# Odd mixer's output projection made from split products, with its parts spread over the attention units; two small reorderings elsewhere

## The reference, cut to what matters

```
# even layer: state space group and differential attention side by side
y_a = mamba2_group(...)            # gated, RMS-normalized over 1024 features
y_b = diff_attention_group(...)    # 8 heads x 4 query blocks = 32 units
h = h + concat([y_a, y_b]) @ ev_w_out          # 2048 -> 1024
h = h + swiglu(rms_norm(h, norm_ffn[0]), ...)
# odd layer
u, c_q, c_kv, k_rope = split(rms_norm(h) @ od_w_in)
y_c = s5_group(u, ...)             # state space, 512 wide, ends in a gated linear unit
y_d = mla_group(c_q, c_kv, ...)    # q = rms(c_q) @ w_uq, kv = rms(c_kv) @ w_ukv; 8 heads x 4 blocks
h = h + concat([y_c, y_d]) @ od_w_out          # 1024 -> 1024
h = h + swiglu(rms_norm(h, norm_ffn[1]), ...)
out = rms_norm(h, norm_final)
```

## Time and profile before

| | us |
|---|---|
| median of 3 runs (lowest to highest) | 3118.67 (3118.42 to 3120.23) |
| the profiled execution | 3117.89 |
| its span | 3115.7 |
| PE busy in the span | 2978.9 (96%) |
| DVE, ACT, POOL busy | 1382.1, 795.4, 1297.4 |

### The profile page before, as it was taken

One profiled execution on the slowest core, in us unless ns is written; L12 is line 12 of the kernel. 1 busy time (PEld: TensorE's weight loads), 2 busy tenths in 40 slices (PEclk: granted clock), 3 DMA queues, 4 the chain that ended last, 5 costly groups with the idle time before them and its releaser, 6 DMA issues.

```text
span 3115.7 us, 36425 instructions
## 1 busy us (share of the span) xinstructions
PE 2978.9 (96%) x14436; PEld 2265.3 (73%) x14436; DVE 1382.1 (44%) x2281; ACT 795.4 (26%) x1491; POOL 1297.4 (42%) x1070
## 2 busy tenths in 40 slices
PE   8999999999989999998899988999999889999997
PEld 5878777778778777776687655788787545478886
DVE  3312455666463122433746676523726844321113
ACT  3011222221130122211326233232223124232222
POOL 2434223223435633457565543744545300054443
PEclk8999999999999999999999998999999889999999
DMA  7111112223222211123321111232324200232322
GB/s 268 41 41 61 61 62 88 64 76 109 91 71 82 75 51 51 51 81 106 97 75 51 59 50 59 76 99 82 99 91 132 69 29 14 81 108 88 101 84 78
DMA packets 244819, 245.76 MB, mean 79 GB/s; under 512 B 5376, under 2 KB 234624, under 8 KB 244032
## 3 DMA queue, kind: packets, MB, share of 16 engines
q1 hardware_dynamic: 243360, 239.92, 24.0%
q0 software_dynamic: 1312, 3.80, 0.4%
HBM read 235.19 MB, written 7.34 MB: 78 GB/s over the span
## 4 chain that ended last, share of the span: by engine, by line
PE 85%; DVE 10%; issue 1%; ACT 1%; POOL 1%; SPq 1%; DMA 1%; DVEq 0%; POOLq 0%; ACTq 0%
PE psum L921 21%; PE psum L923 20%; PE psum L922 20%; PE psum L1178 4%; PE psum L1280 3%; PE psum L1147 2%; PE psum L1115 2%; PE psum L1116 1%; DVE columns L2540 1%; PE psum L1127 1%; PE psum L1077 1%; POOL columns L3232 1%; PE psum L1631 1%; PE psum L1182 1%; PE psum L1426 1%
## 5 line engine op out<-in xcount | busy, mean ns | idle before, releaser
L921 PE MATMUL psum<-columns,columns 128*128 128x512 f32 (+1 forms) x3400 | 1333.7, 392 | 55.2 <-POOL columns L3232 13.6
L923 PE MATMUL psum<-columns,columns 128*128 128x512 f32 (+1 forms) x3400 | 1243.4, 366 | 0.0
L922 PE MATMUL psum<-columns,columns 128*128 128x512 f32 (+1 forms) x3400 | 1242.1, 365 | 0.0
L3232 POOL TENSOR_TENSOR columns<-columns,columns 128x512 fp32r<-128x512 f32 (+1 forms) x660 | 883.8, 1369 | 437.4 <-ACT columns L1799 404.6
L3228 POOL TENSOR_TENSOR columns<-columns,columns 128x512 fp32r<-128x512 f32 x376 | 392.8, 1075 | 1282.7 <-PE psum L923 989.5
L921 PEld LDWEIGHTS psum<-columns,columns 128*128 128x128 f32 x3400 | 646.1, 190 | 236.1 <-issue 99.5
L922 PEld LDWEIGHTS psum<-columns,columns 128*128 128x128 f32 x3400 | 647.2, 190 | 119.8 <-issue 28.5
L923 PEld LDWEIGHTS psum<-columns,columns 128*128 128x128 f32 x3400 | 645.2, 190 | 109.4
L1799 ACT ACTIVATE columns<-columns 128x1024 fp32r<-128x1024 f32 (+2 forms) x154 | 136.8, 936 | 170.4 <-PE psum L923 166.0
L2540 DVE SCALAR_TENSOR_TENSOR columns<-columns,columns,columns 128x256 f32<-128x256 f32 x224 | 149.8, 714 | 0.5
L2522 DVE SCALAR_TENSOR_TENSOR columns<-columns,psum 128x512 f32<-128x512 f32 x80 | 54.8, 685 | 173.6 <-PE psum L1178 169.2
(11 more groups left out here) (405 smaller groups left out, 2805.7 us busy)
## 6 DMA issues: line engine op xcount, KB each, us to landing
columns<-in_w_merge SPq DMA_DIRECT2D x32, 1024.0 KB, 6.1
columns<-in_w_ada SPq DMA_DIRECT2D x24, 1024.0 KB, 5.3
columns<-in_w_in SPq DMA_DIRECT2D x22, 1024.0 KB, 5.3
columns<-in_ev_w_in SPq DMA_DIRECT2D x22, 1024.0 KB, 5.2
columns<-in_ffn_gate SPq DMA_DIRECT2D x22, 1024.0 KB, 5.3
columns<-in_ffn_up SPq DMA_DIRECT2D x22, 1024.0 KB, 5.3
columns<-in_ffn_down SPq DMA_DIRECT2D x16, 768.0 KB, 4.7
columns<-in_ffn_down SPq DMA_DIRECT2D x16, 640.0 KB, 4.3
```

The lines of the kernel that those rows point to most:

```text
L921: mm(dst, weights(0, k), moving(0, k), start=start and k == 0, stop=False)
L922: mm(dst, weights(0, k), moving(1, k), start=False, stop=False)
L923: last = mm(dst, weights(1, k), moving(0, k), start=False, stop=stop and k == k_tiles - 1)
L3232: last = g.tensor_tensor(low[:, c], raw[:, c], high[:, c].bitcast(F32), ALU.subtract)
```

## The change

**The output projection becomes a split product and begins earlier.** `od_out` leaves the list of unsplit stages, so its 64 slices are three fp32r matmuls each, its four panels are split by POOL (both parts), and its input is split tile by tile. ACT writes the high part of each tile (`out_tile`) at the odd mixer's places 12, 20, 22 to 25 and 28, and of the last one behind place 34. The low parts of `yd` are DVE's (`out_low`, places 13, 21, 29 and the end), those of `yc` are POOL's, between the splits of the first and the second panel. From place 28 on, two slices follow each place on PE (14 in all: tiles 4, 5, 0, 1, 2, 3, 6 of outputs 0 and 1). Behind the last place come slice 7 of outputs 0 and 1, then outputs 2 to 7 with all eight. The PSUM banks are 2 to 5 in place of 0 to 3. SP reloads the residual ahead of the third panel in place of the second.

```diff
-WHOLE = ("ada", "od_low", "glu", "od_out")
+WHOLE = ("ada", "od_low", "glu")
+OUT_HIGHS = (4, 5, 0, 1, 2, 3, 6, 7)
+EARLY_AT = 28
+EARLY = [(n, k) for k in OUT_HIGHS[0:7] for n in range(2)]
...
-        program += some("unit", u) + beside.get(u, [])
+        program += some("unit", u) + beside.get(u, []) + some("early", *range(2 * (u - EARLY_AT), 2 * (u - EARLY_AT) + 2) if u >= EARLY_AT else ())
...
# SP
-                if j == 1:
+                if j == 2:
                     sp.wait_ge(x_spilled, 32)
                     sp.wait_ge(scored2, 64)
                     sp.dma_start(xT[:, :, 0:SEQ], x_dram).then_inc(x_loaded, 16)
...
# PE
+                def out_product(n, k, start, stop):
+                    w = split_ready(PANEL0["od_out"] + n // 2)
+                    if n == 0 and k < 4:
+                        pe.wait_ge(y_split, KD + k + 1)
+                    elif n == 0:
+                        pe.wait_ge(od_split, KD + k - 3)
+                    low = yc_low[:, k, :] if k < 4 else yd_low[:, k - 4, :]
+                    src, o = (out_high[:, k, :], low), (2 + n % 4) * BANK
+                    return product(psum[:, o:o + SEQ], ..., lambda part, _: src[part], 1, start, stop)
...
                 pe.wait_ge(p2_ready, 64)
-                    feature_job(n % 4, w, n % 2 * P, lambda k: yc[:, k, :] if k < 4 else yd[:, k - 4, :]).then_inc(gemm_done, 1)
+                    tiles = OUT_HIGHS[7:] if n < 2 else OUT_HIGHS
+                    for k in tiles:
+                        last = out_product(n, k, n >= 2 and k == tiles[0], k == tiles[-1])
+                    last.then_inc(gemm_done, 1)
...
# ACT
+                        if i in (12, 20, 28):
+                            out_tile(4 + (i - 12) // 8)
+                        elif 22 <= i < 26:
+                            out_tile(i - 22)
+                out_tile(7)
...
# POOL
+            for n in range(4):
+                q = PANEL0["od_out"] + n
+                pool.wait_ge(gemm_done, DONE[q - 2 if n >= 2 else PANEL0["od_in"] + 3 + n])
+                split((SPLITS[q] - 1) % 2, KD * PANEL, *panel(q), SPLITS[q])
+                if n == 0:
+                    for k in range(4):
+                        pool.wait_ge(od_high, KD + OUT_HIGHS.index(k) + 1)
+                        g.tensor_tensor(yc_low[:, k, :], yc[:, k, :], out_high[:, k, :].bitcast(F32), ALU.subtract).then_inc(y_split, 1)
```

```diff
-                    if QK_STEPS <= step < QK_STEPS + KD:
-                        i = step - QK_STEPS
+                    if QK_STEPS - KD < step <= QK_STEPS:
+                        i = step - QK_STEPS + KD - 1
                         act.wait_ge(normed_ready, KD + i + 1)
+                        if i < KD - 1:
+                            act.wait_ge(tile_free, i + 1)
+                        else:
+                            act.wait_ge(gemm_done, JOB0["ev_qk"] + 16)
                         f(y_parts[0][:, i, :], xbc[:, i, :], ACT.Copy).then_inc(y_high, 1)
```

More of the change, by code:

```diff
@@ L526, in build @@
         yc = take(4, SEQ, at=A + 17664)
+        out_high = parts(KD, SEQ, at=(A + 6656,))[0]
+        yc_low, yd_low = (place(A + at, (4, SEQ), F32R) for at in (17664, 2048))
         qm, km = xT[:, :, 0:SEQ], take(MLAH, SEQ, at=h_at + 2048)
@@ L668, in build @@
         hid_high = sem("hid_high")
-        s5_arg = sem("s5_arg")
+        tile_free = sem("tile_free")
         s5_exped = sem("s5_exped")
@@ L1515, in ev_qk_out @@
                         last.then_inc(gemm_done, 1)
+                    elif n == 15:
+                        last.then_inc(tile_free, 1)
                 for i in range(4):
@@ L2921, in s5_phases @@
                 yield from reduce_angle(S(2), S(7))
-                dve.drain().then_inc(s5_arg, 1)
+                dve.drain().then_inc(angle_ready, 1)
             def s5_factors():
```

64 lines of the change are left out of this document (35 added, 29 removed).

## The result

| | before | after |
|---|---|---|
| median (lowest to highest), us | 3119.22 (3118.42 to 3120.23), 4 runs | 3092.35 (3088.47 to 3095.02), 4 runs |
| ratio, 95% interval | | 0.9913 (0.9896 to 0.9930) |
| the profiled execution, its span | 3117.89, 3115.7 | 3088.47, 3086.6 |
| PE busy in the span, granted clock | 2978.9, 0.977 | 2964.7, 0.981 |

The changed kernel is 26.9 us faster by medians; 3092.7 was predicted.

A forecast was written before the change was run, and what follows sets the result against it. PE, busy for 2978.9 of 3115.7 us, was taken as the bound. Gains of 13.2 + 11.0 + 1.8 = 26.0 us led from 3117.9 to 3091.9, as a median 3092.7, forecast 3087 to 3099 (0.62), range 3083 to 3106.

The forecast's parts named there:

- Part 1: Output projection: split slices, begun earlier, with POOL splitting the panels, gain 13.2 us, bounds 5 and 18.
- I let the pauses vanish: From place 28: 3.9 us of PE pauses disappear because early slices give the ACT and DVE copies time to finish.
- The join's wait: Behind the last place: PE waits about 1.0 us for the last tile's copy, high part and low part.
- The 2.0 for panel 0's split: Places 18 to 20: POOL's split slows DVE instructions and PE waits, a cost of 2.0 us, bounds 0 and 5.
- At the FFN's start 1.0: Start of the second FFN: DVE finishes two tiles beside POOL, a cost of 1.0 us, bounds 0 and 3.
- The cover is between 0 and 1.4 us, and I take no wait: Output projection: POOL splits each panel within PE's two jobs of 11.1 us, so PE does not wait.
- Part 2: Even layer: low parts made 7 or 8 steps earlier bring the transposes forward, gain 11.0 us, bounds 17 and 4.
- the lead that I took off: Even layer: transposes come 12 us earlier, but 11.0 was taken since the unit behind starts with less lead.
- The rival of moved pauses: Even layer: the pauses only move, so 3 us are gained and the time is 3101; chance 0.12.
- Part 3: Odd layer's low-rank squares: the 7.70 us pause goes but DVE is late next, gain 1.8 us, bounds 9.7 and -2.
- The rival in which DVE's tables run fast enough for PE to bound the part: Odd layer's input projection: 8 us come instead of 1.8, time 3086; chance 0.10.
- The rival of 5 in 100: Place 28 to the end: PE stays at 1.2 GHz, slower, 3149 over the whole stretch; chance 0.05.

The follow-up runs named there:

- p1_alone: Kernel before with only the split output projection, begun at place 28: median 3104.18 us, -12.6 against before.
- 9: Changed kernel with its 14 early slices put where PE waits (3 behind places 24, 27 and 31, 5 behind 34): 3085.31 us.
- Run 4: Changed kernel with its 14 early slices moved from places 28 to 34 to behind the last place: 3093.94 us.
- run 5: The changed kernel itself, unchanged, measured again: 3093.72 us (3089.80 to 3098.22).
- 6: Changed kernel with two more GpSimd instructions before the split of each of the projection's third and fourth panels: 3094.78 us.
- p2_alone: Kernel before with only the even layer's change, the state space result split eight steps earlier: median 3105.09 us, -11.7 against before.
- p3_alone: Kernel before with only the odd layer's change, tiles of their own for the low-rank squares: median 3113.93 us, -2.9 against before.
- 7: Changed kernel with VectorE's key scaling, rotated-key copy and last output table (3 instructions) behind the first, second and third rotations: 3078.70 us.
- 8: Changed kernel with the edits of 7, but four output tables (12 instructions) late, and the small swap matmul behind job 7 instead of 6: 3074.14 us.
- 10: Changed kernel with the edits of 8 and 9 together: 3069.36 us (3068.42 to 3072.82, 5 runs).

## Why the prediction was right, point by point

**Part 1: 13.2 predicted, 12.6 by p1_alone's median, 14.2 from place 28 to the FFN in the profile.** What it named is there: slices of three matmuls in place of the earlier trace rows, the join, no wait for a landing panel. "I let the pauses vanish" was wrong by 1.5: the one at place 28 itself remained (1.49 us), since the first early slices stand behind it; 9 shows that it can go. Run 4 shows how little the placing gave: 0.9 us of waits. The join's wait, 1.0 predicted, was 0.69. It is this chain (DVE, after, with ACT's 0.63 from 2661.19 between):

```profile
2660.47 0.69 DVE L3219 COPY columns<-psum 128x512 f32<-128x512 f32 x1 [6.29 <-PE psum L1638]
2661.86 0.69 DVE L3166 TENSOR_TENSOR columns<-columns,columns 128x512 fp32r<-128x512 f32 x1 [0.69 <-ACT columns L2224]
```

The 50 slices took 35.2 us where 34.7 stood: 0.704 each in place of 0.693. So the stretch from place 28 became 14.2 us shorter, not 15.2. The wait of 0.97 at the FFN went as said.

The 2.0 for panel 0's split were not paid: places 18 to 21 took to 0.1 us what they took before, and the places from there to 28 lost 0.3. The split ran from 2599.62 to 2608.9, and the unit's instructions on DVE beside it were these (DVE, after):

```profile
2603.32 0.69 DVE L3152 TENSOR_REDUCE columns<-psum 128x1 f32<-128x512 f32 x1
...
2605.26 1.25 DVE L3162 TENSOR_SCALAR columns<-columns,columns 128x384 f32<-128x384 f32 x1
```

The maximum reads PSUM and kept its 0.69. The weighting took 1.25 (an unhindered one of this shape 0.42), but PE was at work on the mix and the next scores then and did not wait for it. I had charged the lock to both instructions of a unit, and as if each fell on PE's path. The Trainium skill ("SBUF — State Buffer", section on the two separate sides) has contention between engines only at the pair of SBUF ports that VectorE and GpSimd share; the trace agrees: 1.25 on SBUF, nothing on the PSUM read. Where PE did wait for a weighting beside a split, at place 28 (1.22 us long), the pause was 1.49 in place of the 1.34 that run 5 has there: 0.15. At the FFN's start 1.0 was put down for DVE and 0.48 measured.

"The cover is between 0 and 1.4 us, and I take no wait": 6 shows that the cover was at its lower end, 0.4 us at output 4 and none at output 6, which starts 0.2 us late. This step came out right with nothing to spare.

**Part 2: 11.0 predicted, 11.7 by p2_alone's median and at unit 22 onward.** The argument was that DVE's work decides. The estimate counted from 1872.97 and made it 27.4 us of DVE; the transposes came 27.5 us behind the same point (1873.56), in both profiles of the changed kernel and in p2_alone. So the part's own gain is 12.3 us, not 11.0: the lead that I took off was not lost. The two pauses of about 3.5 us that I left were 1.08 and 2.10, and the low clock, which I had taken as not saved, mostly was. The rival of moved pauses is out: its 3 us for this part is far from the interval (8.1 to 16.5 us).

**Part 3: 1.8 predicted, 2.0 in the profile, 2.9 by p3_alone's median (5.0 faster to 0.6 slower).** DVE had no pause from 2402 to 2464, as written. PE's pause did not move behind job 9, though, but to two places: the small swap behind job 6 (3.71, one of the bounds I had named) and the second rotation. That the bound was DVE is shown by 7: with PE's work the same and only DVE's order changed, 5.2 us came free at that swap, and 6.2 more in 8, counted from unit 22, which changed DVE's order and one matmul's place. The rival in which DVE's tables run fast enough for PE to bound the part is out.

**The low clock.** The rival of 5 in 100 did not happen: the slices ran at 1.00 throughout. The Trainium skill ("TensorE: Matmul & The Clock Gate", what is actually happening) also says that the chip judges activity on a beat of its own, which does not start with the kernel, so that the point of change differs from run to run. The trace agrees in kind: the same places at 0.50 for 6 and for 20 us, 5.4 us apart. I had left this out: the profile before was one execution, in which these places had the short form, and its 3 runs within 1.8 us looked like a kernel that doesn't scatter (its 15 runs of a later session went from 3113.11 to 3122.45).

**The sum.** 26.0 predicted, 26.9 in the first session and 23.3 in the repetition. What was charged and not paid (2.0 and 0.5 for locks, 0.3 at the join, 1.3 in part 2) makes 4.1 us, what was paid and not charged (a pause of 1.5, 0.5 of slices) 2.0. Term by term some 28 us were to be expected, and the clock and the start of the even layer scatter by more than the difference. The hit within 0.4 us is luck; what holds is the three mechanisms and each size to 1 or 2 us.

Open: why the clock falls late in some executions and early in others, and whether the kernels of 7 to 10 never have the long form or had it seldom. That fewer pauses make it rarer fits the runs of 7, 8 and 10, but the profiles of before, p1_alone, p2_alone and p3_alone, whose pauses there are as long or longer, have the short form too, and no run held the pauses and changed the clock alone.

## What to carry to other kernels

When PE is busy for 96% and has a few long pauses, ask for each which engine is next late when the releaser named goes. Here it was VectorE with a backlog of work that nobody needed yet, and moving a scaling, a copy and three instructions of a table (then twelve) behind the wait was worth more than the edit that had uncovered it. Independent slices of a later product shorten a pause only where they stand ahead of it, so place them by the profile's idle column, not evenly. Read a term of a few us as the length between two points, each taken in both timelines: medians whose runs scatter by 8 us hide it, and so does a single point, since the same program reached the even layer 4 us earlier or later.

## What the runs showed of the hardware

- A plain fp32 slice of 128 x 512 cost 0.862 us, the three fp32r matmuls that replace it 0.704: the split product with three times the matmuls is the shorter.
- The same 64 matmuls of 16 columns took 8.7 to 11.6 us in the profiles of these kernels, by where the granted clock fell.
- A reordering that took away one pause of 5.2 us lowered the median by 15.0 us (7). Between two single profiles 1.8 of the rest lay in the stretch right behind it and 4.9 some 40 to 170 us later, in places that ran at 0.50 for longer.
- On SBUF beside POOL DVE's low part took 1.76 us, alone 0.63 (a quarter of the 2.50 in the earlier trace rows); its reads of PSUM kept 0.69.
